# A hybrid decoder layer on eight cores: two weight pairs formed later, stored units spread over five tiles

## The reference

```python
proj = einsum('bsd,dc->bsc', x, w_in[l])                      # 1536 columns
xp   = proj[..., :512]
zg   = gelu(proj[..., 512:])                                  # u | v
pooled   = causal_multiscale_pool(xp)                         # trailing means over 2/4/8/16, minus x
pool_out = einsum('bsgc,gcd->bsgd', pooled, pool_w[l]) * pool_scale[l]
sgu_out  = spatial_gating(zg, ...)                            # u * (tril(W_s) LN(v) + b), chunks of 128
mix = einsum('bsc,cd->bsd', concat([pool_out, sgu_out]), w_out[l])
h   = layer_norm(alpha * x + mix, ln1_g[l], ln1_b[l])
gu  = einsum('bsd,df->bsf', h, w_gate_up)                     # gate | up, 2 x 2816
x   = layer_norm(alpha * h + einsum('bsf,fd->bsd', silu(gate) * up, w_down), ln2_g, ln2_b)
```

## Time and profile before

| | us |
|---|---|
| median of 3 runs | 2246.17 |
| the three runs | 2246.17, 2216.03, 2248.02 |
| the profiled execution, its own time | 2217.75 |
| span of its slowest core (core 2) | 2216.2 |
| spans of the eight cores | 2204.8 to 2216.2 |
| busy PE / DVE / ACT / POOL | 2158.5 / 1613.7 / 979.4 / 596.6 |
| mean TensorE clock granted, by core | 0.993 to 0.995 |

### The profile page before, as it was taken

One profiled execution on the slowest core, in us unless ns is written; L12 is line 12 of the kernel. 1 busy time (PEld: TensorE's weight loads), 2 busy tenths in 40 slices (PEclk: granted clock), 3 DMA queues, 4 the chain that ended last, 5 costly groups with the idle time before them and its releaser, 6 DMA issues.

```text
span 2216.2 us, 34816 instructions; the slowest of 8 cores (2204.8 to 2216.2 us)
## 1 busy us (share of the span) xinstructions
PE 2158.5 (97%) x10055; PEld 975.6 (44%) x10104; DVE 1613.7 (73%) x2661; ACT 979.4 (44%) x1569; POOL 596.6 (27%) x605
## 2 busy tenths in 40 slices
PE   7999999999799999999999999999999999999996
PEld 3444444444344444444444444444444444444443
DVE  4778787687678788688767767776866686687757
ACT  3456655576654144415423441553155145415521
POOL 4334424243111060033006001520431062024204
PEclk9999999999899999999999999999999999999999
DMA  9699999999789686569667846756665675467542
GB/s 176 145 258 238 249 260 225 242 268 275 243 181 247 193 219 188 172 188 221 218 193 209 255 176 179 264 196 173 205 243 186 174 260 196 161 191 268 195 150 93
DMA packets 192473, 463.82 MB, mean 209 GB/s; under 512 B 78880, under 2 KB 106144, under 8 KB 192288
## 3 DMA queue, kind: packets, MB, share of 16 engines
q1 hardware_dynamic: 153056, 383.47, 54.2%
q0 software_dynamic: 39232, 78.13, 18.5%
HBM read 379.37 MB, written 114.16 MB: 223 GB/s over the span
## 4 chain that ended last, share of the span: by engine, by line
PE 89%; DMA 5%; issue 2%; DVE 2%; POOL 1%; ACT 1%; DVEq 0%; POOLq 0%; ACTq 0%; SPq 0%
PE ps L940 46%; PE ps L1013 23%; PE ps L727 8%; PE ps L626 4%; PE ps L596 4%; PE ps L643 4%; DMA sb_wx<-w_gu 2%; DMA sb_xT<-xT 1%; DMA scr_gu<-sb_wr 1%; DMA scr_n<-sb_hop 1%; POOL sb_rst L565 1%; PE ps L686 1%; ACT sb_zr L1081 0%; POOL sb_zr L1083 0%; DVE sb_hop L451 0%
## 5 line engine op out<-in xcount | busy, mean ns | idle before, releaser
L940 PE MATMUL ps<-sb_hop,sb_wx 128*128 128x512 f16 x3500 | 789.1, 379 | 5.1 <-DVE sb_sl L925 3.4
L940 PEld LDWEIGHTS ps<-sb_hop,sb_wx 128*128 128x128 f16 x3500 | 340.0, 98 | 423.1 <-issue 18.9
L1013 PE MATMUL ps<-sb_wx,sb_aop 128*128 128x512 f16 x1764 | 395.1, 379 | 1.6 <-DVE sb_zr L1003 1.6
L940 PE MATMUL ps<-sb_hop,sb_wr 128*128 128x512 f16 x1428 | 339.4, 379 | 4.1 <-ACT sb_u L880 2.1
L565 POOL TENSOR_TENSOR sb_rst<-sb_rst,sb_nhalf 128x1 f32<-128x1 f32 (+1 forms) x96 | 102.6, 1071 | 861.3 <-DVE sb_rst L563 860.4
L880 ACT ACTIVATE sb_u<-ps 128x512 f32<-128x512 f32 x352 | 206.4, 595 | 200.9 <-PE ps L940 199.7
L925 DVE TENSOR_TENSOR sb_sl<-ps,sb_u 128x512 f32<-128x512 f32 x176 | 121.1, 688 | 212.8 <-PE ps L940 182.1
L1013 PEld LDWEIGHTS ps<-sb_wx,sb_aop 128*128 128x128 f16 x1764 | 172.0, 98 | 211.2 <-issue 4.9
L1081 ACT ACTIVATE sb_zr<-sb_zr,sb_rst 128x1024 f32<-128x1024 f32 x62 | 70.5, 1147 | 392.1 <-POOL sb_rst L565 379.6
L880 ACT ACTIVATE ps<-ps 128x512 f32<-128x512 f32 x240 | 139.0, 581 | 179.2 <-PE ps L940 120.1
L940 PEld LDWEIGHTS ps<-sb_hop,sb_wr 128*128 128x128 f16 x1428 | 138.3, 98 | 175.9 <-issue 12.2
(11 more groups left out here) (91 smaller groups left out, 2345.4 us busy)
## 6 DMA issues: line engine op xcount, KB each, us to landing
sb_wx<-scr_gu SPq DMA_DIRECT2D x100, 896.0 KB, 7.3
sb_wx<-scr_dn SPq DMA_DIRECT2D x63, 896.0 KB, 6.0
sb_wr<-scr_gu SPq DMA_DIRECT2D x40, 896.0 KB, 7.6
sb_hr<-x SPq DMA_DIRECT2D x64, 512.0 KB, 15.0
scr_z<-sb_hr SPq DMA_DIRECT2D x64, 512.0 KB, 12.7
sb_zr<-scr_z SPq DMA_DIRECT2D x64, 512.0 KB, 3.6
out<-sb_zr POOLq DMA_DIRECT2D x56, 512.0 KB, 8.8
sb_wr<-scr_dn SPq DMA_DIRECT2D x25, 896.0 KB, 5.8
```

Source lines behind the costliest of these rows:

```text
L940: i_ = e.matmul(ps[:, bk.home, :], lhsT=wv_(u["s"])[:, APOS[m], k * 128:(k + 1) * 128], rhs=hop[:, BPOS[m], k, :], start=(k == 0 and m in ...
L1013: i_ = e.matmul(ps[:, bks[b_].home, :], lhsT=aop[:, AP2[m], j, b_ * 128:(b_ + 1) * 128], rhs=wv_(s)[:, o, :], start=(m in (1, 7) and j == ...
```

## The change

`LATE` goes from 16 to 20, so that `early` holds 11 down units and only pair 0 of gate-up: 13 units. Pairs 1 and 2 are formed in the feed-forward stage. The 13 units are placed at even distances: positions 100, 150, ... 700, which is one unit at the start of each of the mixer tiles 2 to 14, paced by that tile's first v-product. In `fetch_gu` the tile in which a pair is stored becomes min((10 - j) // 2, 4): pairs 9 and 10 in tile 0, 7 and 8 in tile 1, 5 and 6 in tile 2, 3 and 4 in tile 3, 1 and 2 in tile 4. Until a pair is stored, each tile forms it anew. So the tiles form 20, 16, 12, 8 and 4 units.

```diff
-LATE = 16
+LATE = 20
 ...
         def fetch_gu(u, pos, T):
             if u not in done:
                 j = u % NP
-                keep = T == (0 if j >= NP - 4 else 2 if j >= NP - 6 else 3)
+                keep = T == min((NP - 1 - j) // 2, 4)
                 if keep:
                     done.add(u)
                 return prep(u, pos - 1.0, store=keep, pace=["O7"] * (T == 0 and 0 < j < 4))
 ...
         early = [2 * NP + j for j in range(NP)] + [u for j in range(NP - LATE // 2) for u in (j, NP + j)]
         at = {}
         for i, u in enumerate(early):
-            at.setdefault(FIRST + i * (NMT - 1 - FIRST) // len(early), []).append(u)
+            pos = (FIRST - 1) * STEP + i * (NMT - FIRST) * STEP / len(early)
+            at.setdefault(int(pos // STEP), []).append((u, pos % STEP))
         for m in range(NMT):
             mixer(m)
-            for i, u in enumerate(at.get(m, ())):
-                prep(u, STEP * m + 12 * i, False, [f"{'VUP'[i]}{m % 2}"])
+            for u, d in at.get(m, ()):
+                prep(u, STEP * m + d, False, [f"{'V' if d < 10 else 'U' if d < 20 else 'P'}{m % 2}"])
                 done.add(u)
```

## The result

The changed kernel takes 2263.8 us, the median of 4 runs (2255.83 to 2283.15), against 2245.84 us for the kernel before beside it (4 runs, 2216.03 to 2248.02). The ratio is 1.0193, with a 95% interval of 1.0111 to 1.0274. The ratio is taken over runs without a die that is over 1% longer than the other at a lower clock, so it isn't the quotient of the two medians. The kernel is slower, clear of the noise, where no difference was forecast; whether by 2% the interval doesn't tell. The 2263.8 itself lies inside the predicted range. The profiled execution took 2267.38 us, with a span of 2265.8 us on its slowest core.

A forecast was written before the change was run, and what follows sets the result against it. PE, busy 97%, was taken as the bound, with some 25 us idle; -5.3 + 0.5 + 2 - 1.5 + 6 = +1.7 us on the 2246.2 median gave about 2248 us, range 2210 to 2268.

The forecast's parts named there:

- What bounds the kernel: Whole kernel: PE busy 97% of the span; gains only where it stands, some 25 us of 2216, 1.1%.
- Mixer: Mixer stretch 406 to 440: POOL's 13.27 us store wait goes; gain 5.3 us, less 0.5 for the earlier first unit.
- Change of stage: Before tile 0: new loads and additions for pairs 1 and 2 lose 2 us, bounds 0 and 12.
- rival C: Change of stage: DVE waits for new loads before the last projection additions, 10 to 12 us lost; chance 0.12.
- Tile 0: Feed-forward tile 0: four more units formed, four fewer stores; gain 1.5 us, bounds 3.1 and -3.
- Tiles 1 to 4: Feed-forward tiles 1 to 4: added loads, additions and moved stores lose 6 us, bounds 0 and 17.
- Rival B: Ends of tiles 0 to 3: additions pile up and meet POOL's, 8.4 us each, 34 in all; chance 0.15.
- the sign: Tile ends: a POOL wait reaching PE through ACT would make the prediction wrong in kind; no size given.
- The hold: Tile ends: POOL's SBUF reads hold DVE's two-input operations, up to 1.7 us per overlap; the sum used median additions.
- The profiled-level sum: Whole kernel: all terms together add 1.7 us to the profiled 2217.75, giving 2219.5.

The follow-up runs named there:

- e16: The kernel before with only the even placing: 17 mixer units, old tiles of storing; 2234.8 us against 2249.16, ratio 0.9994.
- e6: Changed kernel, but pairs 1 and 2 stored in tile 0 and, in tiles 1 to 4, brought by POOL's loads without additions; 2286.34 to 2574.16 us.
- e5: Changed kernel, but pairs 1 and 2 stored in tile 0, read back in tiles 1 to 4 with their additions repeated; 2358.47 to 2468.11 us.
- e15: Changed kernel with two POOL memsets in place of POOL's addition of line 1083 in tiles 0 to 3; 2629.18, 2499.07 and 2233.36 us.
- e4: The kernel before, unchanged, run once more on a chip with a low clock; 2477.31 us.
- e3: Changed kernel with the old storing rule, so pairs 1 to 4 are all stored in tile 3; 2489.41 us against 2477.31 for the kernel before.

## Why the prediction was wrong

**What bounds the kernel: right.** PE is without work only in few places, and the whole matter stayed within tens of us.

**Mixer: right in mechanism, and the gain came.** The wait of the earlier trace rows is gone: 3.7 us of PE's waits, and the clock of that stretch is 1.00. e16, with all 17 units, has the same 40 us of 40 busy there, so four units fewer are not needed for it. The even placing alone brings it, which the prediction didn't separate.

**Change of stage: the wrong sign.** I took 2 us lost and a floor of 0. The wait for line 743, 7.3 us in the earlier trace rows, fell to 1.1. In the 44 us ahead of tile 0 PE stood 6.8 us (core 1), where I had named 15, and the clock was 0.96, not 0.84. The nine loads were issued in one block from 554.41, 5.63 us of POOL, and line 776 behind them first came at 568.42 and had waited for DVE, so nothing stood. e16 has the same begin of tile 0 (575.4 us) without the forming of pairs 1 and 2, so the new work there is free, and rival C falls. The table's -9.6 against -2.8 is mostly this term. Why line 743 came earlier I did not single out; it came with the even placing.

**Tile 0: -1.5, as predicted**, though by a spread of 7 us over cores the agreement says little.

**Tiles 1 to 4: this step failed**, the term for the tile ends. "I take 1.0 for tile 1 ..., 1.5 for tile 2, 1.0 for tile 3 ..., 2.5 for tile 4. 6 us lost; bounds 0, and ... 17". They lost 6.5, 5.5, 3.1 and 12.7: 27.8 us, outside my bounds. The prediction had the pieces. Rival B named the place and the collision, and put it at 8.4 us per tile end, 34 in all: nearer than the sum, though its own working was off too. It counted only POOL's hits on new additions at 1.7 us each, the hold of the earlier trace rows. Three things were not in it:
- A hold is not bounded by one POOL operation. When two additions stand back to back, one DVE operation can be held for both: 5.46 us for line 1069. The earlier trace rows shows a single addition beside it and I took that as the price.
- The hold reaches PE through ACT. I wrote the sign down (a wait of POOL that reaches PE through ACT) as what would make the forecast wrong in kind, and gave POOL's eight loads per tile end no price of their own. e6 shows that they cost 4 to 5 us a tile without a single new addition, by the very waits that the changed kernel has (15.3 us in ten, against 15.1). In tile 4 there is a load of 22 us beside it, and 8.6 us of PE; there I had taken 2.5.
- I subtracted 5.0 us of free DVE time per tile end. A mean of free time is no cover for an engine that works in order, when the late operation stands ahead of the one that PE needs.

The two costs don't add (e5 7 to 11 us, e6 4 to 5, both 3 to 6.5 in tiles 1 to 3). The planner's lists differ between these kernels, so other operations meet; that this is the reason is argued and not shown. How much of the loss is DVE's holding and how much POOL's fuller list stays open too (e15).

**The hold.** A DVE operation with two SBUF inputs that began during POOL's additions took 5.46 us, and with fills in place of them no line 451 passed 436 ns. The Trainium skill (page "SBUF — State Buffer", section "Who interferes with whom") says that DVE's second SBUF input and a GpSimd operation that reads SBUF exclude each other, and that one that only writes doesn't take part. By that rule the trace agrees. The prediction named the hold, agreed with it, and then summed the additions at their median all the same; rival B was the forecast that used it.

**The time.** The profiled-level sum was +1.7; on an ordinary core it was +12.9: -9.6 - 1.5 + 27.8 - 3.2 = +13.5 from the table's medians. That the median still fell into my range is luck in part: the start gained 6.8 us more than I had said, the range was 58 us wide, and 27.8 us of loss at the tile ends were not in it. The measured ratio's further part comes from the slowest of eight cores and from the 159 us stretches, as the first section says. Whether the change brings the 159 us stretches on more often stays open; four runs can't tell.

## What to carry to other kernels

Before moving work of one engine to a place, look at what the neighbour that shares its port does there, and bound the price of a meeting by the neighbour's longest run of back-to-back operations, not by one operation and not by the median. Free time as a mean is no cover in a list worked off in order: ask which operation that frees a bank stands behind the moved one, on the moved engine and one engine further on. And split a change into its parts before adopting it: here the even placing alone brings the gain, and the rest takes it away.

## What the hardware showed beside it

- One DVE operation of 1.28 us was held to 5.46 us by two POOL additions of together 4.66 us, and POOL's pair in turn took 5.0 to 6.0 us where DVE's operations fell into it (984.79, 999.15). The kernel before has pairs too, and no hold over 2.97 us: what counts is when the DVE operation begins.
- A stall that hides on a slow chip shows on a fast one. Tile 3 of the kernel before takes 202.1 us at the full clock and 198.3 corrected, like its neighbours, at a granted clock of 0.90 (e4, cores 0 to 3). A comparison on such a chip can miss stalls of this size; some of e3's showed.
- Where one core of eight meets a stretch of 159 us at a granted clock of 0.81, the time is some 25 to 30 us longer (by the mean clocks: 2244 to 2250 us and not 2214 to 2216 for the kernel before); a 13 us change is better read from the spans of the other cores than from the times.
